# 512-column products for gate and up, input projections moved beside the substitution, and the attention's head norms and rotation moved off VectorE

## What is computed

```python
qb = _axial_rope(_rmsnorm(qb.reshape(b, l, ATT_HEADS, ATT_HD), q_norm_w), pos_row, pos_col)
kb = _axial_rope(_rmsnorm(kb.reshape(b, l, ATT_KV_HEADS, ATT_HD), k_norm_w), pos_row, pos_col)
ob = _latent_attention(qb, kb, vb, kb_c, vb_c, sink)
y = sigmoid(ga) * (ya @ w_proj_a) + sigmoid(gb) * (yb @ w_proj_b);  x = x + gate * (y @ w_out)
```

```python
h = _rmsnorm_2(x) * (1.0 + sc1) + sh1
x = x + HALF_STEP * g1 * ((silu(h @ w_gate) * (h @ w_up)) @ w_down)     # 1024 -> 2816 -> 1024
```

## Time and profile before

| what | value |
|---|---|
| time, median of 3 runs | 1714.55 us (1713.25 to 1716.82) |
| the profiled execution: time, span | 1717.84 us, 1715.9 us |
| busy PE, PEld (weight load), DVE, ACT, POOL | 91%, 72%, 57%, 35%, 12% |
| chain that ended last, by engine | PE 78%, DVE 10%, ACT 6%, DMA 2% |
| median landing of the mods' weights, of a bias | 6.3 us, 7.3 us |
| gate and up, four times | 500 to 633, 896 to 1028, 1114 to 1247, 1510 to 1645 us |

### The profile page before, as it was taken

One profiled execution on the slowest core, in us unless ns is written; L12 is line 12 of the kernel. 1 busy time (PEld: TensorE's weight loads), 2 busy tenths in 40 slices (PEclk: granted clock), 3 DMA queues, 4 the chain that ended last, 5 costly groups with the idle time before them and its releaser, 6 DMA issues.

```text
span 1715.9 us, 21713 instructions
## 1 busy us (share of the span) xinstructions
PE 1566.3 (91%) x8944; PEld 1231.6 (72%) x8944; DVE 978.8 (57%) x1482; ACT 604.1 (35%) x945; POOL 205.0 (12%) x205
## 2 busy tenths in 40 slices
PE   7997869888889999899989998799998999989998
PEld 2646446545469997785459996699977865489986
DVE  0477775844147777355337776467776453275444
ACT  2425121132034443262234443444433531153442
POOL 0021142000001110043001110011100240001100
PEclk9998969998989999999989999999999999989999
DMA  9444323133347869332338887377976323457551
GB/s 343 141 128 146 98 75 123 59 126 122 123 146 264 282 229 359 130 123 92 106 111 269 265 288 276 116 247 257 311 281 217 123 74 111 147 178 227 185 172 49
DMA packets 192105, 305.44 MB, mean 178 GB/s; under 512 B 6139, under 2 KB 116487, under 8 KB 191879
## 3 DMA queue, kind: packets, MB, share of 16 engines
q1 hardware_dynamic: 189088, 299.45, 51.5%
q10 hardware_dynamic: 2919, 4.61, 0.7%
...
## 4 chain that ended last, share of the span: by engine, by line
PE 78%; DVE 10%; ACT 6%; DMA 2%; issue 2%; POOL 1%; ACTq 0%; DVEq 0%; POOLq 0%
PE ps L380 76%; DVE accs L521 2%; PE ps L383 2%; DVE wlo L1955 1%; ACT whi L1913 1%; DMA ring<-in_w_mod_dram 1%; DMA ring<-in_ffn_w_down_dram 1%; DVE arena L1212 1%; DVE arena L1209 1%; DVE H L1802 1%; DVE H L1736 1%; ACT arena L1447 0%; DVE misc L1514 0%; ACT hhi L1918 0%; DMA ctab<-in_consts_dram 0%
## 5 line engine op out<-in xcount | busy, mean ns | idle before, releaser
L1955 DVE TENSOR_TENSOR wlo<-ring,whi 128x1024 fp32r<-128x1024 f32 x264 | 322.5, 1225 | 221.9 <-ACT whi L1913 215.1
L380 PE MATMUL ps<-hhi,whi 128*128 128x256 f32 x1408 | 406.5, 289 | 20.9 <-DVE hlo L1961 14.9
L380 PE MATMUL ps<-hlo,whi 128*128 128x256 f32 x1408 | 402.0, 286 | 0.0
L380 PE MATMUL ps<-hhi,wlo 128*128 128x256 f32 x1408 | 401.9, 285 | 0.0
L1913 ACT ACTIVATE whi<-ring 128x1024 fp32r<-128x1024 f32 x264 | 274.8, 1055 | 314.4 <-PE ps L380 281.1
L380 PEld LDWEIGHTS ps<-hhi,whi 128*128 128x128 f32 x1408 | 274.4, 195 | 23.4 <-DVE hlo L1961 21.7
L380 PE MATMUL ps<-ring,H 128*128 128x512 f32 (+1 forms) x608 | 266.7, 589 | 13.5 <-ACT arena L1007 6.1
L380 PEld LDWEIGHTS ps<-hlo,whi 128*128 128x128 f32 x1408 | 274.2, 195 | 1.7 <-issue 1.7
L380 PEld LDWEIGHTS ps<-hhi,wlo 128*128 128x128 f32 x1408 | 274.0, 195 | 0.0
L380 PEld LDWEIGHTS ps<-ring,H 128*128 128x128 f32 x608 | 114.6, 195 | 134.1 <-issue 116.8
L521 DVE SCALAR_TENSOR_TENSOR accs<-ring,misc,accs 128x512 f32<-128x512 f32 x266 | 201.3, 757 | 2.7
...
## 6 DMA issues: line engine op xcount, KB each, us to landing
...
```

Source lines behind the costliest of these rows:

```text
L380: return self.e.matmul(o, lhsT, rhs, start=start, stop=stop)
L1955: v.done(v.e.tensor_tensor(lo, M.slot(key)[:, r0:r0 + rn, :], plain(hi), ALU.subtract), ("split", l, sub, n), *([M.freed(key)] if ends els ...
```

## The change

The feed-forward. `HHI` and `HLO` become the halves of one tensor `HH`, so that one product of the high weight takes both (512 columns: the left half is hi·hi, the right half hi·lo), and one of 256 columns adds lo·hi to the left half. Gate and up get a bank each, of six instead of four. The exchange gets two more operations for each block: ScalarE copies the right halves of both banks (512 elements), VectorE adds the left halves, then silu, multiply and rounding as before, now from SBUF. The exchange moves ahead of the group's fourth piece on ScalarE and VectorE.

The delta stage. The order of the rest parts becomes 1, 2, 0, 3, 4, and fourteen of their twenty ticks instead of eight come before y5; part 0 uses banks 6 and 7. Eight of the mods' ticks move from the attention into the chunk steps. SyncE fetches the four parts first, then the mods.

The heads. `v_prepare` goes. ScalarE takes the squares of one head at a time with an accumulated sum (`kb` in `act_state`, `qb` in `act_delta`), and GpSimd does the power, the norm and the rotation (`pool_heads`; `kb` at the start of `pool_state`, `qb` in `pool_delta`). The scratch is in `gates`, so the load of one gate's bias waits for the fence "delta".

```diff
@@ -160,7 +160,7 @@
 NS = 5
-POOLS = {"all": range(8), "six": range(6), "mods": (6, 7), "rest": (0, 1), "att": (2, 3, 4, 5), "bo": (7,), "row": (6,), "sq": (4, 5, 6, 7), "low": (0, 1), "skk": (2,), "mod3": (3,), "sdec": (4, 5), "sq2": (6, 7), "ga": (0, 1, 2, 3),
+POOLS = {"all": range(8), "six": range(6), "mods": (6, 7), "rest": (0, 1), "att": (2, 3, 4, 5), "bo": (7,), "row": (6,), "sq": (4, 5, 6, 7), "low": (0, 1), "skk": (2,), "mod3": (3,), "sdec": (4, 5), "sq2": (6, 7), "ga": range(6),
@@ -193,7 +193,8 @@
         self.WHI, self.WLO = self.sbr("whi", [128, 4, 1024]), self.sbr("wlo", [128, 4, 1024])
-        self.HHI, self.HLO = self.sbr("hhi", [128, 8, 256]), self.sbr("hlo", [128, 8, 256])
+        self.HH = self.sbr("hh", [128, 2, 8, 256])
+        self.HHI, self.HLO = self.HH[:, 0, :, :], self.HH[:, 1, :, :]
@@ -442,7 +443,7 @@
     ends = {2: ("residual", "first"), 5: ("residual", 0, 0), 8: ("residual", 0, 1)}
-    free = {5: ("fence", "delta"), 8: ("fence", "delta")}
+    free = {2: ("fence", "delta"), 5: ("fence", "delta"), 8: ("fence", "delta")}
@@ -814,6 +815,7 @@
     a.done(a.e.activation(M.ea, M.w_alog, ACT.Exp), ("ea",))
+    act_head_squares(a, "kb", M.KB, 4, 2, ("kvb",))
@@ -895,6 +897,8 @@
         g.done(g.e.memset(c, 0.0), ("cb clear",))
+    g.wait_ge(("in", "tab"), ("in", "bc"))
+    run(pool_heads(g, "kb", M.KB, 4, 2, M.w_kn, (2, 3)))
@@ -941,19 +945,21 @@
             g.done(g.e.tensor_tensor(t, t, over(M.C[mask], 2), ALU.mult), ("kqm",))
-    g.wait_ge(("tok out", 1))
+    g.wait_ge(("tok out", 1), ("head squares", "qb"))
...
     g.done(g.e.tensor_tensor(M.NEGC[:, :, 4:8], M.NEGC[:, :, 4:8], M.BETA[:, :, 4:8], ALU.mult), ("negb",))
+    queries = pool_heads(g, "qb", M.QB, 2, 8, M.w_qn, (0, 1), M.QR)
+    tick(queries)
...
                    ("kdec", n, d))
-        if n < 2:
-            pool_rstd(g, ("kb", "qb")[n], 8 + 8 * n)
+        if n == 0:
+            run(queries)
@@ -994,7 +1000,7 @@
     for n in part:
-        yield from pe_tok(pe, ("rest", n), 256, "rest")
+        yield from pe_tok(pe, ("rest", n), 256, "mods" if n == 0 else "rest")
@@ -1008,12 +1014,10 @@
 def sp_delta(sp, mods):
-    run(sp_rest(sp, [1, 2]))
+    run(sp_rest(sp, [1, 2, 0, 3]))
+    tick(mods, 16)
+    run(sp_rest(sp, [4]))
     tick(mods, 8)
-    rest = sp_rest(sp, [3, 4, 0])
-    tick(rest, 1)
-    tick(mods, 8)
-    run(rest)
@@ -1046,7 +1050,7 @@
     M = pe.M
-    fill = pe_rest(pe, [1, 2, 3, 4, 0])
+    fill = pe_rest(pe, [1, 2, 0, 3, 4])
@@ -1059,7 +1063,7 @@
             tick(fill, 1)
-    tick(fill, 6)
+    tick(fill, 12)
@@ -1096,7 +1100,6 @@
             pe_blocks(pe, ("y6", s, d), 64, pairs, 64)
-    tick(fill, 1)
@@ -1124,6 +1127,7 @@
             pe.done(ins, ("vn", n, d))
+        tick(mods, 3)
@@ -1152,15 +1156,17 @@
     act_rest(a, 1, ("dd read", 9), ("dd read", 7))
+    act_head_squares(a, "qb", M.QB, 2, 8, ("rest out", 1), ("hrs", "kb"))
+    act_rest(a, 2)
...
         a.done(a.e.activation(blocks(M.F, b, 0, b), turned(M.TX, b, 0), ACT.Copy), ("blocks",))
-    act_rest(a, 2)
...
                ("y5 out", s, 0), ("free", key))
+    act_rest(a, 0, ("blocks",))
@@ -1178,7 +1184,7 @@
                ("x6 out", s), ("free", key))
-    for n in (3, 4, 0):
+    for n in (3, 4):
@@ -1239,7 +1245,7 @@
 def v_delta(v, mods):
-    M, prep = v.M, v_prepare(v)
+    M = v.M
@@ -1279,7 +1285,7 @@
                                                 src[:, blk, h, :], ALU.mult, ALU.add), ("rhs", n, d), ("free", key))
-        tick(prep, 1)
+        tick(mods, 1)
@@ -1300,7 +1306,7 @@
                 v.done(ins, ("free", key), ("o raw", n, d))
-        tick(prep, 2)
+        tick(mods, 1)
@@ -1316,9 +1322,6 @@
             v.done(v.e.tensor_tensor(M.O[:, ch, :], M.O[:, ch, :], M.ps(key), ALU.add), ("free", key), ("o", n, d))
-        if not ends:
-            tick(prep, 1)
-    run(prep)
@@ -1354,17 +1357,46 @@
-def v_rope(v, src, nh, c_, s_, ax, tmp):
...
+def act_head_squares(a, name, xv, nb, nh, *after):
+    M, n = a.M, 0
+    a.wait_ge(*after)
+    for b in range(nb):
+        for h in range(nh):
+            a.done(a.e.activation(M.gates[:, 3, n * 64:n * 64 + 64], xv[:, b, h * 64:h * 64 + 64], ACT.Square,
+                                  accum_out=M.ssb[:, n:n + 1]), ("head squares", name))
+            n += 1
+    a.wait_ge(("head squares", name))
+    a.done(a.e.activation(M.ssb[:, 0:n], M.ssb[:, 0:n], ACT.Identity, bias=M.epsc, scale=1.0 / 64), ("hms", name))
+def pool_heads(g, name, xv, nb, nh, wv, roped, out=None):
+    M = g.M
+    g.wait_ge(("hms", name))
+    g.op(g.e.tensor_tensor(M.rsb[:, 0:nb * nh], M.ssb[:, 0:nb * nh], M.half[:, 0:nb * nh], ALU.pow), ("hrs", name))
+    for b in range(nb):
+        x3 = xv[:, b, :].rearrange("p (h d) -> p h d", d=64)
+        g.op(g.e.tensor_tensor(x3, x3, M.rsb[:, b * nh:(b + 1) * nh].unsqueeze(2).broadcast_to([128, nh, 64]), ALU.mult))
+        g.op(g.e.tensor_tensor(x3, x3, over(wv, nh), ALU.mult))
+    tmp = M.gates[:, 1, :].rearrange("p (b n) -> p b n", b=2)[:, :, 0:nh * 64]
+    for blk in range(2):
+        c_, s_ = M.C["r1c"][:, blk * 64:blk * 64 + 64], M.C["r1s"][:, blk * 64:blk * 64 + 64].rearrange("p (a f) -> p a f", a=4)
+        x, t4 = xv[:, roped[blk], :], tmp[:, blk, :].rearrange("p (h a f) -> p h a f", h=nh, a=4)
+        x4, x3 = x.rearrange("p (h a f) -> p h a f", h=nh, a=4), x.rearrange("p (h d) -> p h d", d=64)
+        for i in range(4):
+            g.op(g.e.tensor_tensor(t4[:, :, i, :], x4[:, :, i ^ 1, :], s_[:, i, :].unsqueeze(1).broadcast_to([128, nh, 16]), ALU.mult))
+        g.op(g.e.tensor_tensor(x3, x3, over(c_, nh), ALU.mult))
+    yield
+    for blk in range(2):
+        x3, t3 = (t.rearrange("p (h d) -> p h d", d=64) for t in (xv[:, roped[blk], :], tmp[:, blk, :]))
+        if out is None:
+            g.op(g.e.tensor_tensor(x3, x3, t3, ALU.add), ("roped",))
+            continue
+        for kv in range(2):
+            g.done(g.e.tensor_tensor(out[:, blk, :, kv * 64:kv * 64 + 64], x3[:, kv * 4:kv * 4 + 4, :], t3[:, kv * 4:kv * 4 + 4, :], ALU.add),
+                   ("roped",))
+    yield
@@ -1460,40 +1492,6 @@
-def v_prepare(v):
...
@@ -1884,13 +1883,14 @@
         for q in range(4):
+            if q == 3:
+                yield f
...
                 tick(work, beside(f, q))
-        yield f
@@ -1904,7 +1904,7 @@
     M = a.M
-    SG = spare(M)[0:3]
+    SG = spare(M)
@@ -1928,25 +1928,32 @@
     for f in split_all(a, l, sub, emit, None):
-        for j in range(2 if isinstance(f, int) else 0):
-            i, key = (f + j) % 3, ("gu", l, sub, f + j)
-            a.wait_ge(("gu", l, sub, f), ("alo", l, sub, f + j - 3))
-            a.done(a.e.activation(SG[i], M.ps(key)[:, 0:256], ACT.Silu), ("silu", l, sub, f + j))
+        pair = range(f, f + 2) if isinstance(f, int) else ()
+        for x in pair:
+            key = ("gu", l, sub, x)
+            b = M.banks[key, 0]
+            a.wait_ge(key, ("alo", l, sub, x - 3))
+            a.done(a.e.activation(SG[x % 3], M.psum[:, b:b + 2, 256:512], ACT.Copy), ("copied", l, sub, x))
+        for x in pair:
+            a.wait_ge(("summed", l, sub, x))
+            a.done(a.e.activation(SG[x % 3][:, 0, :], SG[x % 3][:, 0, :], ACT.Silu), ("silu", l, sub, x))
+        for j, x in enumerate(pair):
+            i = x % 3
             a.wait_ge(("act", l, sub, f + j))
-            a.done(a.e.activation(M.AHI[:, f + j, :], SG[i], ACT.Copy), ("ahi", l, sub, f + j))
+            a.done(a.e.activation(M.AHI[:, f + j, :], SG[i][:, 0, :], ACT.Copy), ("ahi", l, sub, f + j))
...
     M = g.M
-    SG = spare(M)[0:3]
+    SG = spare(M)
...
         g.wait_ge(("ahi", l, sub, f))
-        g.op(g.e.tensor_tensor(M.ALO[:, f, :], SG[f % 3], plain(M.AHI[:, f, :]), ALU.subtract), ("alo", l, sub, f))
+        g.op(g.e.tensor_tensor(M.ALO[:, f, :], SG[f % 3][:, 0, :], plain(M.AHI[:, f, :]), ALU.subtract), ("alo", l, sub, f))
...
     M = v.M
-    SG = spare(M)[0:3]
+    SG = spare(M)
@@ -1973,25 +1980,40 @@
             i, key = (f + j) % 3, ("gu", l, sub, f + j)
+            b = M.banks[key, 0]
+            v.wait_ge(("copied", l, sub, f + j))
+            v.done(v.e.tensor_tensor(SG[i], SG[i], M.psum[:, b:b + 2, 0:256], ALU.add), ("summed", l, sub, f + j),
+                   ("free", (key, 0)), ("free", (key, 1)))
+        for j in range(2 if isinstance(f, int) else 0):
+            i = (f + j) % 3
             v.wait_ge(("silu", l, sub, f + j))
-            v.done(v.e.tensor_tensor(SG[i], SG[i], M.ps(key)[:, 256:512], ALU.mult), ("act", l, sub, f + j), ("free", key))
+            v.done(v.e.tensor_tensor(SG[i][:, 0, :], SG[i][:, 0, :], SG[i][:, 1, :], ALU.mult), ("act", l, sub, f + j))
...
     for f in range(0, 22, 2):
-        bs = [pe.bank(("gu", l, sub, f + j), "ga") for j in range(2)]
...
             hi, lo = piece(M, n, 256)
-            o0, k0 = 256 * (q // 2), 4 * (q % 2)
+            k0 = 4 * (q % 2)
...
             for j in range(2):
-                c = slice(j * 128, j * 128 + 128)
```

(20 more changed lines are left out.)

41 lines of the change are left out of this document (1 added, 40 removed).

## The result

After, the time is 1702.3 us in the median of 5 runs (1695.7 to 1704.3); before, beside it, 1714.8. The ratio, which is taken over all runs and not from the two medians (they are 12.5 us apart), is 0.9909, 95% interval 0.9894 to 0.9925: 13 to 18 us faster. The forecast was 1674, with 1659 to 1694: the sign is right, the size is less than half, and the time lies outside the range.

The account below looks back on a forecast made before the run. It took PE as the bound by stages, with VectorE stopping it in the hole and becoming the bound in gate and up. First block -27.9 and feed-forwards -12.4 gave -40.3 from 1717.8: 1677.5, median 1674, range 1659 to 1694.

Parts of the forecast that it names:

- The hole is filled: Delta stage: six projection ticks move into PE's idle 21.11 us before y5, which starts 0.4 us later.
- The two slow ticks become 3.6 (-2.5, -2.1): Delta stage, from y5 to the last x6 copy: two slow projection ticks fall to 3.6 us each.
- Banks 0 and 1 come free by ScalarE's silu: Delta stage: ScalarE's silu of part 2, no longer behind the triangles, frees these banks for the moved ticks.
- rival (b): Hole filled only in part: a slot or bank late, or chunk steps longer; half of -29.6 stays, 1689; chance 0.17.
- Steps "13.2 to 267.7": Delta chunk steps to the fence: step 0 takes 13.2 us, the four sum to 42.4 instead of 61.6, -19.2.
- GpSimd, +2: Delta stage: VectorE's ticks run slower beside GpSimd's head work, six of nine by 0.34 us each; +2 (0 to 10).
- Attention, -1.5: Attention: 16 ticks instead of 24, two of five leave its chain; -1.5 us (-6 to 0).
- Products, 4.7 us a stage if PE is the bound: Gate and up: a triple takes 0.347 instead of 0.360 us, 0.0133 for each of 352 triples.
- VectorE becomes the bound, and the first three stages gain 2.0 us each: Gate and up: VectorE's period averages 11.78 us a group, 130.3 a stage against 132.3; PE alone would need 127.6.
- The new wait at the start of down, "covered": Down, first and third stage: new 2 to 2.6 us bank wait, hidden by ScalarE's wait for down weights' DMA.
- Fourth stage -5.9: Fourth feed-forward: gate and up gain 3.9 us with 16 ticks only, and down's banks come free 2.0 sooner.
- (e): Rival: product distances stay at 0.36 us a triple, with the exchange longer; 1685; chance 0.04.

Follow-up runs that it names:

- part-4 run: After, with the last projection part (part 4) in the two banks of the mod sums; 1691.6 us, 0.9848 to before.
- hole alone: Before, with only projection tick order, part 0's banks and ScalarE's copies as in after, head norms still on VectorE; 1710.0 us, 0.9970.
- ticks-last runs: Six gate-and-up mod ticks moved beside down's splits: before 1696.4 us, after 1679.1, after with part 4's banks changed and down's banks taken late 1665.8.
- after with three products: After, with six of eight wide products issued as two of 256 columns; 1701.1 us, 0.9916 to before.

## Why the prediction was right or wrong, step by step

- **The hole is filled**: right, PE's 21.11 us of waiting are 0.74, y5 begins 0.9 us later than before (0.4 forecast) and takes 3.93 us (3.2 less forecast, 2.5 measured).
- **"The two slow ticks become 3.6 (-2.5, -2.1)"**: wrong. They take 5.40 each, as the clock falls to its lower level behind y5 and behind x5 even with the hole filled. I took the full clock of the filled hole for the whole stretch. 3.6 us missing; why the clock falls there stays open.
- **"Banks 0 and 1 come free by ScalarE's silu"**: right for part 0, but part 4 needs banks that part 3 holds, and ScalarE's copy of part 3 stands behind the last x6 copy. I followed the banks of the moved parts and not of the part behind them. That cost 2.89 us and, by the clock behind the stop, 2.5 more, and the part-4 run gave these 5.4 back. With the attention, which is 5 us shorter in every kernel with that edit, it gave 10.5: the largest single step that failed. It is a piece of my rival (b), a bank that comes late.
- **Steps "13.2 to 267.7", then 29.2 to the fence**: from the state copies of step 0 to the fence 51.1 us before, 33.5 after; -17.6 of the forecast -19.2, so this step held. What is missing up to the fence lies before it: the last x6 copy ends at 259.35 and not at 254.5, by the slow ticks and y5, and step 0 is 4.4 us longer, by the stop in front of part 4. That `v_prepare` would have been on the path was right: the steps take 45.3 us with it (hole alone).
- **GpSimd, +2**: its effect on a tick is there (4.10 us for three ticks at 245.99, 1.37 each, against 0.74 alone), but PE runs without a stop from 230.75 to 257.68, so it cost nothing. By the Trainium skill (SBUF — State Buffer, "SBUF: two separate sides") one of the two is blocked for the whole length of the other's operation, where VectorE's has two inputs in SBUF, as a tick has; the 1.37 us agree with it in kind. Gate and up can't tell, since hardly an operation of the two overlaps there.
- **Attention, -1.5**: not there (+0.6), at a clock of 0.90 in the stretch. With part 4 in other banks it is -5.0 against before (168.3), at 0.95.
- **Products, 4.7 us a stage if PE is the bound**: mis-sized. It is 3.4, and more triples fell to the lower clock in this profile, where they gain nothing (nine against six, +1.3). I took the wide product's 0.227 us from the down product; beside the narrow one it is 0.233. By the Trainium skill (TensorE: Matmul & The Clock Gate, "Back-to-back issue gap") the fixed part, which the page gives for an isolated product, would have made it 0.9, so neither my 13 ns nor the page's 2.5 ns holds; a triple gained 10.
- **"VectorE becomes the bound, and the first three stages gain 2.0 us each"**: this failed in the feed-forwards. I gave each engine its own period and took the longer. In truth PE, ScalarE and VectorE wait for each other in turn: VectorE idles 0.81 us for ScalarE in one group, PE 1.39 for VectorE in another. The first stage takes 130.9 us with most of VectorE's ticks left out and 133.5 with all of them, from PE's first start to its last end. Against before the four stages changed by +0.4, +0.6, -0.9 and -2.2 us, -2.0 in all where -9.9 was forecast. "PE never stops" in gate and up was also not so in before: in the fourth stage it waits 2.8 us for VectorE's ticks.
- **The new wait at the start of down, "covered"**: right in kind. The wait came (2.14, 3.9 and 2.8 us), and taking it away gave nothing; but what covered it was not needed, as the ticks-last runs show. In the second feed-forward the down product itself is 3.9 us longer than before (71.6 against 67.8, at a granted clock of 0.93 against 0.98), which the sum did not have; the other kernels with the feed-forwards' change and the ticks of before took 69.2 to 72.7 us there, all above 67.8.
- **Fourth stage -5.9**: -5.6, in part by luck. Gate and up gave 2.2 us and not 3.9, the wait at their end 1.9 as forecast (2.0), and down 1.6 that the sum did not have, at a granted clock of 1.00 instead of 0.97.
- **Mixers**: not in the sum. They are 4.9 us longer at a granted clock of 0.97 and 0.96 against 0.97 and 0.98, with the same instructions; over the runs a mixer takes either 189.6 or about 192 us, and after with three products had 189.6 twice, so these 4.9 us are the profile's and not the change's.

The sum was -40.3; by the profile the first block missed 10 us, the feed-forwards 11 (8 in gate and up, 3 at the start of down and in it) and the mixers 5. So two steps of mine failed: that the banks of the projections come free in time, where the runs show a stop at part 4 worth 10.5 us, and that the longer of two engines' periods is the stage's, where the runs show waits in turn and a floor of PE 2.2 us under before instead of 4.7. The falls of the clock behind y5 and x5 (3.6 us) are seen and not explained. Rivals (b) and (e) each named a piece; none had all at once, and the range left no room for two shortfalls together.
